# Gathering the tokens of two experts at a time, in two fp32r parts, and moving the gates' arithmetic

## The reference, cut to what matters

```python
logits = h @ w_router + b_router            # 256 x 8
top_val, top_idx = lax.top_k(logits, 2)     # two experts for each token
gates = softmax(top_val)
# expert e, for its tokens:  y = (silu(h @ w_gate[e]) * (h @ w_up[e])) @ w_down[e]
# w_gate, w_up: 1024 x 1408, w_down: 1408 x 1024
# h_out = x + sum over a token's two experts of gate * y, then a last RMS norm
```

## Time and profile before

| | before |
|---|---|
| median of three runs | 2189.7 us (2188.58 to 2191.74) |
| the profiled execution's own time | 2185.39 us |
| its span, first to last instruction | 2183.6 us |
| PE busy | 2049.4 us, 94% |
| VectorE busy | 1310.1 us, 60% |
| ScalarE busy | 1051.6 us, 48% |
| mean granted TensorE clock | 0.956 |

### The profile page before, as it was taken

One profiled execution on the slowest core, in us unless ns is written; L12 is line 12 of the kernel. 1 busy time (PEld: TensorE's weight loads), 2 busy tenths in 40 slices (PEclk: granted clock), 3 DMA queues, 4 the chain that ended last, 5 costly groups with the idle time before them and its releaser, 6 DMA issues.

```text
span 2183.6 us, 33486 instructions
## 1 busy us (share of the span) xinstructions
PE 2049.4 (94%) x13860; PEld 1757.7 (80%) x13860; DVE 1310.1 (60%) x1988; ACT 1051.6 (48%) x1692; POOL 256.9 (12%) x270
## 2 busy tenths in 40 slices
PE   6999999999999899999999878999897999999997
PEld 4776678888788765899988878999886788888886
DVE  1338535666544447577556554544466588888886
ACT  2336523333333335466545424444435467676774
POOL 0301113010100320132111321110100000000000
PEclk9999999999999899999999898999998899999998
DMA  7332343454322111245543103455451488888783
GB/s 299 121 135 97 145 165 118 172 182 164 116 77 94 67 58 58 87 166 184 204 152 138 38 23 125 174 185 183 155 213 62 153 314 323 326 303 328 303 328 146
DMA packets 52670, 364.85 MB, mean 167 GB/s; under 512 B 5920, under 2 KB 8224, under 8 KB 8864
## 3 DMA queue, kind: packets, MB, share of 16 engines
q1 hardware_dynamic: 49488, 357.06, 44.1%
q10 hardware_dynamic: 3024, 5.58, 0.7%
HBM read 361.57 MB, written 1.05 MB: 166 GB/s over the span
## 4 chain that ended last, share of the span: by engine, by line
PE 84%; DVE 8%; issue 3%; ACT 3%; POOL 2%; DMA 1%; SPq 0%; DVEq 0%; POOLq 0%; ACTq 0%
PE ps L77 22%; PE ps L78 21%; PE ps L79 21%; PE ps L74 18%; DVE WLO L91 3%; PE ps L82 2%; ACT R L85 1%; DVE SM L105 1%; POOL R L91 1%; DVE R L91 1%; DMA ring<-W 1%; POOL h L95 1%; ACT WHI L85 1%; DVE x L88 0%; DVE h L88 0%
## 5 line engine op out<-in xcount | busy, mean ns | idle before, releaser
L91 DVE TENSOR_TENSOR WLO<-ring,WHI 128x1024 fp32r<-128x1024 f32 x557 | 670.8, 1239 | 208.7 <-ACT WHI L85 208.0
L85 ACT ACTIVATE WHI<-ring 128x1024 fp32r<-128x1024 f32 x557 | 568.1, 1052 | 121.9 <-PE ps L79 118.8
L77 PE MATMUL ps<-HHI,WHI 128*128 128x256 f32 (+1 forms) x1680 | 549.1, 327 | 29.8 <-DVE HLO L88 15.0
L78 PE MATMUL ps<-HLO,WHI 128*128 128x256 f32 (+1 forms) x1744 | 560.9, 322 | 0.0
L79 PE MATMUL ps<-HHI,WLO 128*128 128x256 f32 (+1 forms) x1680 | 541.9, 323 | 0.0
L77 PEld LDWEIGHTS ps<-HHI,WHI 128*128 128x128 f32 x1680 | 330.6, 197 | 68.2 <-issue 38.1
L78 PEld LDWEIGHTS ps<-HLO,WHI 128*128 128x128 f32 x1744 | 343.1, 197 | 20.6
L79 PEld LDWEIGHTS ps<-HHI,WLO 128*128 128x128 f32 x1680 | 330.3, 197 | 21.7
L74 PE MATMUL ps<-R 64*64 64x64 f32 (+9 forms) x2736 | 227.8, 289 | 5.1 <-ACT R L85 2.1
L74 PEld LDWEIGHTS ps<-R 64*64 64x64 f32 (+4 forms) x2736 | 170.1, 157 | 46.6 <-issue 37.6
L85 ACT ACTIVATE R<-ps,VEC 128x512 f32<-128x512 f32 (+1 forms) x106 | 69.3, 659 | 255.8 <-PE ps L79 253.6
(11 more groups left out here) (171 smaller groups left out, 2863.4 us busy)
## 6 DMA issues: line engine op xcount, KB each, us to landing
ring<-W SPq DMA_DIRECT2D x340, 1024.0 KB, 4.9
x<-xt ACTq DMA_DIRECT2D x1, 2048.0 KB, 14.8
CR<-const_nsa ACTq DMA_DIRECT2D x1, 560.0 KB, 4.9
out<-x SPq DMA_DIRECT2D x1, 512.0 KB, 3.1
out<-x ACTq DMA_DIRECT2D x1, 512.0 KB, 3.0
CR<-const_rw ACTq DMA_DIRECT2D x1, 448.0 KB, 3.2
CR<-const_gqa ACTq DMA_DIRECT2D x1, 320.0 KB, 17.0
CR<-const_mla ACTq DMA_DIRECT2D x1, 320.0 KB, 2.9
```

The costliest lines, as they stand in the source:

```text
L77: self.e.matmul(out, l[0], r[0], start=start, stop=False)
L78: self.e.matmul(out, l[0], r[1], start=False, stop=False)
L85: return self.e.activation(out, in_, func, **kw)
L91: return self.e.tensor_tensor(out, in0, in1, op)
```

## The change

The turned tokens are kept in two fp32r parts: ScalarE rounds each of the four banks to HTHI (one copy, as before for HT) and VectorE subtracts to HTLO (`tokens_low`, four new instructions). The places of two experts stand side by side in one matrix PPR of 256 columns, in fp32r (zeros and ones are exact in it), and `gather(p)` multiplies first HTHI and then HTLO by it, in eight banks of 512 columns (two feature tiles each). ScalarE copies the banks of the HI half to XSP[0], VectorE copies those of the LO half to XSP[1], with no subtraction. XSP now holds one pair, so its filling waits until the second expert of the last pair has had its last up product. Gathers are made at i = 1, 3 and 5, beside the first.

The transposes of the places become products with an identity in fp32r (IDM), and the products with the gates run on two parts of the gates; both are now in `spread(p)`, behind the up product of block 0 of each even expert. The gates' arithmetic (`gates_dve`) stands behind VectorE's copies of the first gather. VectorE makes the places of the two coming experts in blocks 0 and 1 of each odd expert. Nothing else differs: the products of the experts, the scatters and the weights' stream are the same.

```diff
@@ -561,12 +561,18 @@
     HHI = over("HHI", "R2", 7168, 4096, F32R)[:, :].rearrange("p (j n) -> p j n", n=512)
     HLO = over("HLO", "h", 0, 4096, F32R)[:, :].rearrange("p (j n) -> p j n", n=512)
     HHM = over("HHM", "R2", 8192, 2048, F32R)[:, :].rearrange("p (j n) -> p j n", n=256)
-    XSP = [over("XS" + n, "R1", 2048 * i, 2048, F32R)[:, :].rearrange("p (a k n) -> p a k n", a=2, k=8)
+    XSP = [over("XS" + n, "R1", 2048 * i, 2048, F32R)[:, :].rearrange("p (k n) -> p k n", k=8)
            for i, n in enumerate(("HI", "LO"))]
+    HTP = [over("HT" + n, "R1", 4096 + 2048 * i, 2048, F32R)[:, :].rearrange("p (c n) -> p c n", c=2)
+           for i, n in enumerate(("HI", "LO"))]
+    PPR = over("PPR", "R2", 0, 512, F32R)[:, :].rearrange("p (c n) -> p c n", c=2)
     HDP = [[over("HD%s%d" % (n, j), of, col + 1408 * i, 1408, F32R)[:, :].rearrange("p (k n) -> p k n", n=128)
...
     YSP = [over("YS" + n, "R2", 3584 + 2048 * i, 2048, F32R)[:, :].rearrange("p (a n) -> p a n", n=1024)
+           for i, n in enumerate(("HI", "LO"))]
+    IDM = over("IDM", "R2", 7688, 128, F32R)[:, :]
+    GGP = [over("GG" + n, "R2", 7816 + 16 * i, 16, F32R)[:, :].rearrange("p (c n) -> p c n", c=2)
            for i, n in enumerate(("HI", "LO"))]
     DHI = over("DHI", "R2", 2048, 1024, F32R)[:, :].rearrange("p (a n) -> p a n", a=2)
     DLO = over("DLO", "R2", 3072, 1024, F32R)[:, :].rearrange("p (a n) -> p a n", a=2)
@@ -2990,7 +2996,6 @@
     lg, gg, mk, pos = (rows3(W4[:, 16 * i:16 * i + 16], 8) for i in range(4))
     oh1, oh2, tmp = (rows3(W4[:, 64 + 16 * i:80 + 16 * i], 8) for i in range(3))
     rm, RB = W4[:, 112:124], W4[:, 128:136]
-    HT = R1[:, 6144:8192].rearrange("p (c n) -> p c n", c=2)
     order8 = row3(CR[:, 384:392], 2)
     before, SEL8 = CR[:, 256:384], CR[:, 392:400]
     LR = R2[:, 9600:9856]
@@ -3009,7 +3014,7 @@
         t.then_inc(*did("group", ("router_t",), *closes(p)))
         for c in range(2):
             for half in range(2):
-                b = take(pe, ("ht", c, half), ("ht", c, half))
+                b = take(pe, ("ht", c, half), ("htlo", c, half))
                 for k in range(4):
                     t = pe.transpose(b[:, 128 * k:128 * k + 128], H(4 * half + k)[:, 128 * c:128 * c + 128], ident)
                 t.then_inc(*did("turned", ("ht_t", c, half)))
@@ -3035,8 +3040,8 @@
         for c in range(2):
             for half in range(2):
                 a.wait_ge(*at("ht_t", c, half))
-                a.act(HT[:, c, 512 * half:512 * half + 512], bank("ht", c, half)[:, :], ACT.Copy).then_inc(
-                    *did("tokens", ("ht", c, half)))
+                a.act(HTP[0][:, c, 512 * half:512 * half + 512], bank("ht", c, half)[:, :], ACT.Copy).then_inc(
+                    *did("tokens", ("hthi", c, half)))
         a.wait_ge(*at("gap"))
         a.act(rm[:, 2:4], rm[:, 2:4], ACT.Exp).then_inc(*did("exp", ("gap_exp",)))
@@ -3062,28 +3067,48 @@
         top(tmp, oh2, rm[:, 2:4])
         v.tt(mk, oh1, oh2, ALU.add).then_inc(*did("route", ("two",)))
         v.tt(rm[:, 2:4], rm[:, 2:4], rm[:, 0:2], ALU.subtract).then_inc(*did("route", ("gap",)))
+        tokens_low(v, 0)
         v.wait_ge(*at("place"))
         step(v.cp, pos, rows3(bank("place")[:, 0:16], 8))
-        places_dve(v, 0, 0)
+        for e in range(2):
+            places_dve(v, 0, e)
+        tokens_low(v, 1)
+        step(v.rmax, rm[:, 8:9], bank("place")[:, 16:24])
+        v.cp(FLAG[:, :], rm[:, 8:9]).then_inc(*did("flag", ("flag",), ("flag0",)))
+    def tokens_low(v, c):
+        for half in range(2):
+            z = slice(512 * half, 512 * half + 512)
+            v.wait_ge(*at("hthi", c, half))
+            v.tt(HTP[1][:, c, z], bank("ht", c, half)[:, :], HTP[0][:, c, z], ALU.subtract).then_inc(
+                *did("tokens_lo", ("htlo", c, half)))
+    def gates_dve(v):
+        def step(op, *a, **kw):
+            op(*a, **kw).then_inc(*did("route"))
+            v.wait_ge(*last("route"))
         v.wait_ge(*at("gap_exp"))
...
         step(v.tt, oh2, oh2, col3(rm[:, 2:4], 8), ALU.mult)
-        v.tt(gg, oh1, oh2, ALU.add).then_inc(*did("route", ("weights",)))
-        step(v.rmax, rm[:, 8:9], bank("place")[:, 16:24])
-        v.cp(FLAG[:, :], rm[:, 8:9]).then_inc(*did("flag", ("flag",), ("flag0",)))
-    PP = R2[:, 0:512].rearrange("p (a c n) -> p a c n", a=2, c=2)
+        v.tt(gg, oh1, oh2, ALU.add).then_inc(*did("route", ("gates",)))
+        v.wait_ge(*at("gates_hi"))
+        v.tt(GGP[1], gg, GGP[0], ALU.subtract).then_inc(*did("route", ("weights",)))
     GP = R2[:, 7680:7688]
+    def of_pair(e):
+        return slice(128 * (e % 2), 128 * (e % 2) + 128)
     def places_dve(v, r, e):
         if e >= 2:
-            v.wait_ge(*at("gathered", r, e - 2))
+            v.wait_ge(*at("placed", r, e // 2 - 1))
         for c in range(2):
-            t = v.ts(PP[:, e % 2, c, :], CR[:, CAP * r:CAP * r + 128], pos[:, c, e:e + 1], mk[:, c, e:e + 1],
+            t = v.ts(PPR[:, c, of_pair(e)], CR[:, CAP * r:CAP * r + 128], pos[:, c, e:e + 1], mk[:, c, e:e + 1],
                      ALU.is_equal, ALU.mult)
         t.then_inc(*did("places", ("places", r, e)))
@@ -3110,8 +3135,8 @@
             for n, es in enumerate(TOGETHER):
                 if es[-1] == i - 2:
                     scatter(n)
-            if i + 1 < 8:
-                gather(i + 1)
+            if i in (1, 3, 5):
+                gather((i + 1) // 2)
             if 0 <= i - 1 < 8:
                 down(i - 1)
@@ -3128,26 +3153,31 @@
     def experts_pe(pe, r):
         st = L["moe", r]
-        def gather(e):
-            i = e % 2
-            pe.wait_ge(*at("places", r, e))
-            for c in range(2):
-                for half in range(2):
-                    pe.wait_ge(*at("ht", c, half))
-            for half in range(2):
-                b = take(pe, ("gx", r, e, half), ("xlo", r, e, half))
-                for k in range(4 * half, 4 * half + 4):
-                    for c in range(2):
-                        t = pe.mm(b[:, 128 * (k % 4):128 * (k % 4) + 128], HT[:, c, 128 * k:128 * k + 128],
-                                  PP[:, i, c, :], c == 0, c == 1)
-                t.then_inc(*did("group", ("gx", r, e, half)))
-            b = take(pe, ("pgt", r, e), ("pgt", r, e))
+        def gather(p):
+            for e in (2 * p, 2 * p + 1):
+                pe.wait_ge(*at("places", r, e))
+            for i, name in enumerate(("hi", "lo")):
+                for kk in range(4):
+                    b = take(pe, ("gx" + name, r, p, kk), ("x" + name, r, p, kk))
+                    for k in (2 * kk, 2 * kk + 1):
+                        for c in range(2):
+                            pe.wait_ge(*at("ht" + name, c, k // 4))
+                            t = pe.mm(b[:, 256 * (k % 2):256 * (k % 2) + 256], HTP[i][:, c, 128 * k:128 * k + 128],
+                                      PPR[:, c, :], c == 0, c == 1)
+                    t.then_inc(*did("group", ("gx" + name, r, p, kk)))
+        def spread(p):
             pe.wait_ge(*at("weights"))
-            for c in range(2):
-                pe.transpose(b[:, 128 * c:128 * c + 128], PP[:, i, c, :], ident)
-            for c in range(2):
-                t = pe.mm(b[:, 256:257], PP[:, i, c, :], gg[:, c, e:e + 1], c == 0, c == 1)
-            t.then_inc(*did("turned", ("gathered", r, e)))
+            for e in (2 * p, 2 * p + 1):
+                b = take(pe, ("pgt", r, e), ("pgt", r, e))
+                for c in range(2):
+                    pe.mm(b[:, 128 * c:128 * c + 128], PPR[:, c, of_pair(e)], IDM, True, True)
+                for c in range(2):
+                    for i in range(2):
+                        t = pe.mm(b[:, 256:258], PPR[:, c, of_pair(e)], GGP[i][:, c, 2 * p:2 * p + 2], c + i == 0, c + i == 2)
+                t.then_inc(*did("turned", ("gathered", r, e)))
+            S.events["placed", r, p] = S.events["gathered", r, 2 * p + 1]
         def turn(e, nb):
             n = BLOCKS[nb][1] // 128
@@ -3175,10 +3205,12 @@
                 for w in range(2):
                     product(e, up_group(e, nb, w), ("mup", r, e, nb, w),
                             ("silu_m", r, e, nb) if w == 0 else ("hdn", r, e, nb),
-                            lambda k: (XSP[0][:, e % 2, k, :], XSP[1][:, e % 2, k, :]),
-                            lambda k: [("xlo", r, e, k // 4)])
+                            lambda k: (XSP[0][:, k, of_pair(e)], XSP[1][:, k, of_pair(e)]),
+                            lambda k: [("xhi", r, e // 2, k // 2), ("xlo", r, e // 2, k // 2)])
                     if w == 0:
                         turn_after(e, nb, turn)
+                    elif nb == 0 and e % 2 == 0:
+                        spread(e // 2)
         def down(e):
             if e == 7:
@@ -3211,18 +3243,25 @@
         if r:
             hi_units(a, st.first)
-        def gather(e):
-            for half in range(2):
-                a.wait_ge(*at("gx", r, e, half))
-                if e >= 2:
```

(55 more changed lines are left out.)

## The result

The first comparison gave 2171.77 us (median of four runs, 2170.08 to 2175.78) against 2190.34 us for the kernel before: ratio 0.9918, 95% interval 0.9901 to 0.9935. The two profiled executions are closer to the forecast: 2185.39 and 2170.17 us, 15.2 us apart.

The account below looks back on a forecast made before the run. TensorE was taken as the bound, VectorE 84% loaded behind it. Terms -13.5, 0, +0.3, +0.4, -0.5 and +0.4 sum to -12.9 us, applied to the median of earlier runs: 2176.8 us, range 2173.8 to 2182.5.

Parts of the forecast that it names:

- seven gathers gone, three pairs put in: On PE in the expert layer: seven gathers of 3.57 us removed, 96 fp32r products of 0.120 us added, -13.5 us.
- transposes and gates, with the 0.58 that left the start: Six instructions per expert, moved into `spread`, at unchanged cost: term 0; the first 0.58 us moves from start to block 0.
- first expert product sooner: At the start, behind the first gather: first expert product at 1727.7 instead of 1728.02 us, -0.3 us.
- wait behind `spread`, four times: Block 0 of even experts: weights ready about 0.1 us after PE's two-unit runway of 2.72 us, four times, +0.4 us.
- places moved: Places leave block 1 of four even experts (-0.8 us) and enter block 0 of three odd ones (+0.3): -0.5 us.
- boundaries without a gather: Behind up of experts 0, 2, 4, 6, VectorE loses its catch-up pause but has 0.4 us to spare: +0.4 us.
- The gates' chain: Behind the first gather, gates follow VectorE's LO copies; unit 4 ready near 1732.6, wanted at 1733.2 us: hidden, 0.6 to spare.
- applied to that median: Last step: the -12.9 us from the profiled execution applied to the median of the runs shown, giving 2176.8 us.
- the missed pause: Rival, chance 0.15: at four boundaries without a gather VectorE lacks its spare 0.4 us, PE loses 5.5 us; 2182.3 us.
- slow gathers: Rival, chance 0.05: fp32r gather products run at several passes, as float32, above 0.26 us each; 2212 us.
- nothing saved: Rival, chance 0.05: VectorE's cycle doesn't shrink, 25 us of gathers turn into waits for WLO; about 2189.5 us.

Follow-up runs that it names:

- the pauses put back: Changed kernel with 32 products of 256 columns that nobody reads where gathers were removed, behind up of experts 0, 2, 4, 6: 2189.07 us, ratio 0.9996.

## Why the prediction was right or wrong

The terms of the sum against what the two profiled executions show, in us:

| term | forecast | measured |
|---|---|---|
| seven gathers gone, three pairs put in | -13.5 | -13.5 |
| transposes and gates, with the 0.58 that left the start | +0.6 | +0.9 |
| first expert product sooner | -0.3 | -0.2 |
| wait behind `spread`, four times | +0.4 | +1.1 |
| places moved | -0.5 | -0.5 |
| boundaries without a gather | +0.4 | 0 |
| waits behind the seven gathers, gone | none | -2.0 |
| behind the last down product | none | -0.75 |
| sum | -12.9 | -15.0 (the two executions are 15.2 apart) |

**The gathers: the size right, the reason half right.** 224 instructions in 25.0 us became 96 in 11.5. The reason given was that a product pays for its weight load and streams 256 columns in nearly the time of 128. For fp32r this is borne out: 0.111 us at 128 columns, 0.120 at 256, and 0.11 even for the gates' products of 2 columns, so below 256 columns the number of columns is not what costs. That the weight load sets this floor fits, but it was not shown apart from other fixed costs of a product, since every product here loads its weights anew (13732 products and 13732 weight loads in the changed kernel). For float32, the type of the old gather, the reason fails: there 128 columns took 0.112 us and 256 took 0.21, so widening alone gains next to nothing: 6.72 us for a pair in float32 against 2 x 3.57 = 7.14 for two gathers of before.

The formula of the Trainium skill ("TensorE: Matmul & The Clock Gate", section "Back-to-back issue gap"), by which the term would have been -2 us, is given there for an isolated product; for a stream with a weight load before each product the same section gives about 81 ns at 128 columns. The 0.111 us measured here lie above both the 56 ns and the 81.

**The wait in the old order, priced at nothing.** The prediction followed the chain behind the transposes (ScalarE copies their result before it rounds the next weights), noted that the same chain stands in the trace of before, charged it four times for `spread`, and took nothing off for the seven places from which it goes. Each of these cost 0.3 us: at six the 66 down products took 15.25 to 15.30 us instead of 14.99, at the first the 24 up products 5.80 instead of 5.47. All 528 down products fell from 122.1 to 120.4 us. The chain's size was off too: 0.27 us late instead of 0.1 (24 products behind `spread` in 5.74 to 5.76 us instead of 5.47).

**The small terms.** `spread` takes 1.26 us for a pair, 0.63 for an expert instead of 0.58. The places cost the start 0.53 us, and the clock rose at the same moment as before. The gates' chain was hidden. The wait of 0.45 us beside the places fell to 0.28 at four experts; at three odd ones 48 products of block 0 took 11.38 to 11.40 us instead of 11.33.

**The end** is not shown to belong to the change. From the last down product to the end of the span it took 21.2 us before and 20.4 after, but 20.2 and 20.7 in the two repeats of the changed kernel, and 19.1 to 21.2 over all twelve traces. It tends to be shorter the later the clock falls behind that product: 21.2 us with the fall 4.1 us behind it (before), 20.7 with 4.3, 20.2 with 4.9 (the repeats), 19.1 with 6.7 (the pauses put back).

**The step that failed** is the last, "applied to that median", with a range that reached 3 us below it. That width came from the terms alone and held nothing for the medians themselves. The changed kernel's own medians, of four to six runs each with no edit between them, were 2171.8, 2177.1 and 2173.9; the range's lower end, 2173.8, does not cover them. The mis-sized terms, -15.2 us in the profiled pair instead of -12.9, moved the forecast towards that end but would not have crossed it: 2189.7 - 15.2 = 2174.5, and the median of all 15 runs, 2174.65 us, lies inside the range as well. Over all runs the difference is 14.9 us against 12.9 forecast. So the mechanism was nearly right, and the first median fell outside by the scatter of what lies ahead of the layer, for which the sum had no term. Why the clock's low stretches fall differently from one execution to another stays open.

None of the rivals came: the missed pause is refuted by the pauses put back, slow gathers by 0.120 us, nothing saved by the window.

## What to carry to other kernels

On a TensorE-bound stage, cost a product by start-to-start distances of its own form; with new weights for each product, going from 128 to 256 columns in fp32r was nearly free here (0.111 to 0.120 us), and neither the type nor the width gave that alone. When a chain is charged where it is put in, take it off where it goes. Before settling on a change of PE's work, look at how far ahead its feeders are told to run: one more unit of lead gave almost as much as all of this change (12.5 against 14.2 us of the stage). And state a range for the medians that will be compared, not for the stage that was changed.

## What the runs showed of the hardware

With 64 gather products of 128 columns in fp32r back to back, PE was busy without a gap from 1723.54 us, and the granted clock stayed at 0.50 until about 1741.1, 17.6 us, through the gather and the first products of 512 columns behind it. That is one execution. With 32 fp32r products of 256 columns, at the same 0.21 us apart, the clock rose 4.0 us behind their start: 1722.13 to about 1726.1 in the changed kernel, and 4.0 to 4.1 us in its two repeats and in five more traces whose first gather has this form. With the pair in float32, 0.43 us apart at this clock, it rose 4.0 us behind the start, and with the float32 instructions of 128 columns of the kernel before 4.5 us behind it, in two traces. In all of them the clock was already low when the gather began. What sets the rise was not tried.

The distance between the starts of two TensorE products, each with new weights and at clock 1.0, was 0.11 us for 2 and for 128 columns in fp32r, 0.120 for 256 and 0.227 for 512. For the instructions of a float32 product, two of them for each, it was 0.112 us at 128 columns and 0.21 at 256.
